# Where the operands of TensorE start in SBUF: every region at 128 above a multiple of 256 bytes, the low halves at 160, 192 or 224

## The reference

```python
for i in range(2):
    h = rms_norm(x, attn_norm[i])
    c_q, c_kv, k_r, q_d, k_d, v_d, g_mla, g_dil = split(h @ w_in[i])
    o_mla = latent_attention(rms_norm(c_q) @ w_uq[i], rms_norm(c_kv) @ w_ukv[i], k_r)
    o_dil = dilated_attention(q_d, k_d, v_d)             # 3 groups x 8 heads of 64
    merged = sigmoid(g_mla) * (o_mla @ w_br_mla[i]) + sigmoid(g_dil) * (o_dil @ w_br_dil[i])
    x = x + merged @ w_out[i]
    h = rms_norm(x, ffn_norm[i])
    if i == 0:
        x = x + (silu(h @ w_gate) * (h @ w_up)) @ w_down              # 1024 -> 3584 -> 1024
    else:
        x = x + sum_e gates[e] * (silu(h @ wg[e]) * (h @ wu[e])) @ wd[e]   # top 2 of 8 experts
    x = x + sigmoid(rms_norm(x, ple_norm[i]) @ ple_w_gate[i]) * (p[i] @ ple_w_proj[i])
return rms_norm(x, final_norm)
```

## The kernel before

| tile | role | before | mod 256 | after | mod 256 |
|---|---|---|---|---|---|
| hi | streams, lines 1918, 1919 | 65664 | 128 | 65664 | 128 |
| lo | streams, line 1944 | 82048 | 128 | 82112 | 192 |
| hT_hi | stationary | 106624 | 128 | 106880 | 128 |
| hT_lo | stationary | 114816 | 128 | 115136 | 192 |
| hs_hi | stationary | 167168 | 0 | 167808 | 128 |
| hs_lo | stationary | 171264 | 0 | 171968 | 192 |
| eaT_hi | stationary | 179456 | 0 | 180352 | 128 |
| eaT_lo | stationary | 181504 | 0 | 182496 | 224 |
| faT_hi | stationary | 158976 | 0 | 159616 | 128 |
| faT_lo | stationary | 163072 | 0 | 163744 | 160 |
| omT_hi | stationary | 204032 | 0 | 204672 | 128 |
| omT_lo | stationary | 129664 | 128 | 130176 | 128 |
| odT, latT, peT (both halves) | stationary | | 0 | | 128 |

## Time and profile before

### The profile page before, as it was taken

The page is one execution under the profiler, slowest core; times in us unless marked ns, Lnnn a source line. Parts: engine busy times, 40 slices in busy tenths (PEclk is TensorE's granted clock), DMA queues, the critical chain, the costliest instruction groups (busy, mean ns, idle before and its releaser), DMA issues.

```text
span 1835.9 us, 27322 instructions
## 1 busy us (share of the span) xinstructions
PE 1827.4 (100%) x8942; PEld 1506.3 (82%) x8942; DVE 1475.3 (80%) x1707; ACT 1245.2 (68%) x1563; POOL 142.0 (8%) x203
## 2 busy tenths in 40 slices
PE   9999999999999999999999999999999999999998
PEld 8888888888888888788888888888888888888887
DVE  6557876566575558779999999999999999999997
ACT  6556664444355556657777787787777777877776
POOL 2400000000002200011101001001010010010000
PEclk9999999999999999999999999999999999999999
DMA  8543345555546543359999999999999999999993
GB/s 331 213 161 115 124 161 192 183 185 193 186 180 238 186 158 118 115 171 375 378 364 362 376 354 398 353 382 374 361 374 374 368 370 361 377 379 359 402 365 125
DMA packets 74065, 511.33 MB, mean 279 GB/s; under 512 B 8280, under 2 KB 8800, under 8 KB 14352
## 3 DMA queue, kind: packets, MB, share of 16 engines
q1 hardware_dynamic: 69072, 493.25, 70.4%
q0 software_dynamic: 4768, 16.95, 3.2%
q10 hardware_dynamic: 160, 0.27, 0.0%
HBM read 501.53 MB, written 8.91 MB: 278 GB/s over the span
## 4 chain that ended last, share of the span: by engine, by line
PE 99%; DVE 1%; issue 0%; ACT 0%; POOL 0%; DVEq 0%; POOLq 0%; ACTq 0%
PE ps L1918 29%; PE ps L1944 29%; PE ps L1919 29%; PE ps L2407 1%; PE ps L2144 1%; PE ps L2120 1%; PE ps L2096 1%; PE ps L2169 1%; PE ps L1957 1%; PE ps L1959 1%; PE ps L1963 1%; PE ps L2106 1%; PE ps L2154 1%; PE ps L1990 1%; PE ps L2547 0%; PE ps L2430 0%
## 5 line engine op out<-in xcount | busy, mean ns | idle before, releaser
L1230 DVE TENSOR_TENSOR lo<-raw,hi 128x1024 fp32r<-128x1024 f32 (+1 forms) x940 | 1103.1, 1211 | 189.1 <-ACT hi L724 185.4
L724 ACT ACTIVATE hi<-raw 128x1024 fp32r<-128x1024 f32 (+1 forms) x940 | 969.0, 1050 | 335.4 <-PE ps L1944 326.3
L1918 PE MATMUL ps<-hi,hs_hi 128*128 128x512 f32 x896 | 360.4, 402 | 0.0
L1919 PE MATMUL ps<-hi,hs_lo 128*128 128x512 f32 x896 | 352.3, 393 | 0.0
L1918 PE MATMUL ps<-hi,hT_hi 128*128 128x512 f32 (+1 forms) x752 | 298.0, 397 | 0.0
L1919 PE MATMUL ps<-hi,hT_lo 128*128 128x512 f32 (+1 forms) x752 | 291.7, 389 | 0.0
L1944 PE MATMUL ps<-lo,hs_hi 128*128 128x512 f32 x896 | 282.0, 395 | 0.0
L1944 PEld LDWEIGHTS ps<-lo,hs_hi 128*128 128x128 f32 x896 | 168.6, 188 | 40.2
L1944 PE MATMUL ps<-lo,hT_hi 128*128 128x512 f32 (+1 forms) x752 | 200.1, 388 | 0.0
L1918 PEld LDWEIGHTS ps<-hi,hs_hi 128*128 128x128 f32 x896 | 168.6, 188 | 38.2
L1919 PEld LDWEIGHTS ps<-hi,hs_lo 128*128 128x128 f32 x896 | 168.9, 189 | 35.4
(11 more groups left out here) (361 smaller groups left out, 1706.5 us busy)
## 6 DMA issues: line engine op xcount, KB each, us to landing
raw<-in_stream SPq DMA_DIRECT2D x466, 1024.0 KB, 6.1
ybuf<-xs POOLq DMA_DIRECT2D x2, 1024.0 KB, 5.5
raw<-in_stream SPq DMA_DIRECT2D x3, 672.0 KB, 8.7
gain<-in_ffn_norm POOLq DMA_DIRECT2D x2, 512.0 KB, 7.9
gain<-in_ple_norm POOLq DMA_DIRECT2D x2, 512.0 KB, 6.8
hbuf<-hnf POOLq DMA_DIRECT2D x1, 1024.0 KB, 9.1
xs<-ybuf POOLq DMA_DIRECT2D x1, 1024.0 KB, 12.5
out_x<-hnat SPq DMA_DIRECT2D x3, 256.0 KB, 2.1
```

The costliest lines, as they stand in the source:

```text
L724: a.activation(dst, src, ACT.Copy).then_inc(hi_done, 1)
L1230: v.tensor_tensor(dst, src, h, ALU.subtract).then_inc(lo_done, 1)
L1918: pe.matmul(o, ah, wh[:, kk, :], start=(first and kk == 0), stop=False)
L1919: pe.matmul(o, al, wh[:, kk, :], start=False, stop=False)
```

## The change

The instructions of all five engines stay the same and in the same order; no tile, loop, wait or transfer is added or taken away. Only start addresses in SBUF move. `region()` now rounds up to 128 above a multiple of 256, which takes the regions qk_odd, Dr, Mr and Tr and all in them from 0 to 128 mod 256. The filler of 64 bytes ahead of `lo` and of `hT_lo` sets these at 192, and one of 192 bytes behind each brings the next tile back to 128. In Dr three low stationary tiles get an offset of their own: `faT_lo` 32, `hs_lo` 64 and `eaT_lo` 96 above the 128 of the others, and the tiles behind them move up by 256 or 512 bytes so that they keep 128.

```diff
@@ -123,7 +123,7 @@
             return t
 
         def region(n):
-            top[0] = (top[0] + 127) // 128 * 128
+            top[0] = (top[0] + 127) // 256 * 256 + 128
             r = top[0]
             top[0] += n
             return r
@@ -131,10 +131,14 @@
 
         raw = sb("raw", [P, RAW, SLAB])
         hi = sb("hi", [P, RING, UNIT], F32R)
+        top[0] += 64
         lo = sb("lo", [P, RING, UNIT], F32R)
+        top[0] += 192
         xs = sb("xs", [P, T, D])
         hT_hi = sb("hT_hi", [P, KD, S], F32R)
+        top[0] += 64
         hT_lo = sb("hT_lo", [P, KD, S], F32R)
+        top[0] += 192
         gain = sb("gain", [P, D])
         glat = sb("glat", [P, LAT])
         om_at = top[0]
@@ -217,28 +221,28 @@
         f_sig = at("f_sig", [P, T, CH], F32, Dr)
         f_act = at("f_act", [P, T, CH], F32, Dr + 4096)
         faT_hi = at("faT_hi", [P, 4, S], F32R, Dr + 8192)
-        faT_lo = at("faT_lo", [P, 4, S], F32R, Dr + 12288)
+        faT_lo = at("faT_lo", [P, 4, S], F32R, Dr + 12288 + 32)
 
         hn_hi = at("hn_hi", [P, T, D], F32R, Dr)
         hn_lo = at("hn_lo", [P, T, D], F32R, Dr + 8192)
         hs_hi = at("hs_hi", [P, KD, P], F32R, Dr + 16384)
-        hs_lo = at("hs_lo", [P, KD, P], F32R, Dr + 20480)
-        e_sig = at("e_sig", [P, CH], F32, Dr + 24576)
-        e_act = at("e_act", [P, CH], F32, Dr + 26624)
-        eaT_hi = at("eaT_hi", [P, 4, P], F32R, Dr + 28672)
-        eaT_lo = at("eaT_lo", [P, 4, P], F32R, Dr + 30720)
+        hs_lo = at("hs_lo", [P, KD, P], F32R, Dr + 20480 + 64)
+        e_sig = at("e_sig", [P, CH], F32, Dr + 24832)
+        e_act = at("e_act", [P, CH], F32, Dr + 26880)
+        eaT_hi = at("eaT_hi", [P, 4, P], F32R, Dr + 28928)
+        eaT_lo = at("eaT_lo", [P, 4, P], F32R, Dr + 30976 + 96)
         eaT2_hi = at("eaT2_hi", [P, 4, P], F32R, Tr + 16384)
         eaT2_lo = at("eaT2_lo", [P, 4, P], F32R, Tr + 18432)
-        y_hi = at("y_hi", [P, D], F32R, Dr + 32768)
-        y_lo = at("y_lo", [P, D], F32R, Dr + 36864)
+        y_hi = at("y_hi", [P, D], F32R, Dr + 33280)
+        y_lo = at("y_lo", [P, D], F32R, Dr + 37376)
         hnf = at("hnf", [P, T, D], F32, Tr + 8192)
         hsn = at("hsn", [P, D], F32, Tr + 16384)
         ysb = at("ysb", [P, D], F32, Tr)
         hbuf = nc.dram_tensor("hbuf", (S + P, D), F32, kind="Internal").ap()
         ybuf = nc.dram_tensor("ybuf", (S + P, D), F32, kind="Internal").ap()
-        sel = at("sel", [P, T, P], F32R, Dr + 40960)
-        selT = at("selT", [P, S], F32R, Dr + 41984)
-        rt0 = Dr + 43008
+        sel = at("sel", [P, T, P], F32R, Dr + 41472)
+        selT = at("selT", [P, S], F32R, Dr + 42496)
+        rt0 = Dr + 43520
         rw = at("rw", [P, KD, NE], F32, rt0)
         rw_hl = at("rw_hl", [P, KD, 2, NE], F32R, rt0 + 256)
         rb = at("rb", [P, NE], F32, rt0 + 768)
@@ -268,9 +272,9 @@
         idx_in = at("idx_in", [P, 1], U32, rt0 + 1696)
         idx_out = at("idx_out", [P, 1], U32, rt0 + 1728)
 
-        pnat = at("pnat", [P, T, PD], F32, Dr + 49152)
-        peT_hi = at("peT_hi", [P, 2, S], F32R, Dr + 51200)
-        peT_lo = at("peT_lo", [P, 2, S], F32R, Dr + 53248)
+        pnat = at("pnat", [P, T, PD], F32, Dr + 49664)
+        peT_hi = at("peT_hi", [P, 2, S], F32R, Dr + 51712)
+        peT_lo = at("peT_lo", [P, 2, S], F32R, Dr + 53760)
         psg = at("psg", [P, T, D], F32, Dr)
         pp = (o_mla, pp1)
 
```

## The result

The changed kernel takes 1844.7 us (median of 7 executions, 1843.98 to 1845.18) against 1837.89: a ratio of 1.0038, with a 95% interval of 1.0026 to 1.0050. It is slower by 6.8 us, where 28 us less were forecast. The profiled execution has a span of 1843.4 us, 7.5 more than before.

A forecast was written before the change was run, and what follows sets the result against it. The prediction took TensorE's matmul sequence as the bound: 24.5 us from hs and eaT, 1.7 from faT and 1.7 from omT and its like sum to 28, so 1837.7 - 28 = 1809.7, or 1810 us; range 1790 to 1842.

The forecast's parts named there:

- What bounds the kernel: Whole kernel: TensorE's sequence of 8,942 matmuls sets the time, PE busy 1827.4 us of a span of 1835.9.
- Addresses as the cause, by their distance mod 256,: 512-column matmuls: moving read and next stationary load interfere by relative address; equal rests give 226.7 ns, others some 231.7.
- What equal rests would give: Experts' hs and eaT 24.5 us, dense FFN's faT 1.7, omT and three like it 1.7: sum 28 us.
- the pricing of the low halves: Lines 1918, 1919 and 1944: offsets of the low tiles cost nothing, 226.7 ns each, so the sum stays 28 us.
- the 336-column projection: First projection of layer 1: blocks at 192 and 128 alternate at 13.3 ns over 140.0, so 64 above is free.
- `omT` with mixed halves at 232.9 ns: Low tile at 128, high at 0: a third loads at equal rests, yet 7 matmuls take 1.63 us.
- `hT` loses its pattern: Slower: any unequal third spoils all stages; experts stay at 232.8 ns, hT loses 13.5 us, giving 1851; chance 0.18.
- One third stays dear: Line 1918 alone costs 232.8 ns, the other two 226.7: a gain of 14, 1824 us; chance 0.17.
- The change doesn't touch the cause: hT is cheap for lying below byte 131,072, faT, hs and eaT stay above: nothing changes, 1838 us; chance 0.12.
- The prediction's help from `omT_lo`: omT_lo, at 128 mod 256 but nearly all above byte 131,072, was not cheap, which favours the half of memory.
- Better than equal rests: Lines 1918 and 1944: a small distance avoids half of what is over 213.3 ns, another 31 us, 1779; chance 0.08.
- The other engines: Experts: DMA would rise from some 370 to 380 GB/s, VectorE from 93% to 95% busy; both hold, little to spare.

The follow-up runs named there:

- all at 128: The kernel before with region() rounding to 128 above a multiple of 256, no fillers, so all 512-column operands start at 128 mod 256: 1812.94 us.
- all at 0: The kernel before with base moved up by 128 bytes and regions rounded to multiples of 256, every operand at 0 mod 256: 1812.08 us.
- second kernel of distances: Against the changed kernel: hi and lo at 128 mod 256, both halves of hT 64 above, hs 32 above, eaT 96 above, faT 64 below; 1848.38 us.

## Why the prediction was wrong

**What bounds the kernel** was right: in every kernel PE is busy throughout, and steps times counts give the time.

**Addresses as the cause, by their distance mod 256,** was right, and is shown by the kernels with all at 128 and all at 0. The rule of the Trainium skill, page "SBUF — State Buffer", section "Who interferes with whom", that TensorE's two read ports are independent and PE never waits on anyone, is not borne out here: with the same instructions in the same order, addresses alone moved the time between 1812 and 1848 us.

**What equal rests would give** was put at 28 us. With truly equal rests it is 24.7 to 25.5 us. The steady 226.7 ns was the right figure, but after small matmuls or a switch to another tile it takes up to a dozen steps to be reached (in the kernel with all at 128, `hs` has means up to 229.7 ns in the first twelve and 226.7 from the thirteenth on), so the means are 227.0 (`eaT`) and 227.7 (`hs`).

**The step that failed is the pricing of the low halves.** For line 1944 I took "64 above costs nothing there" from the 336-column projection, and for line 1918 I extended it to the other direction. With 512 columns a distance of 64 under line 1944 alone gives 232.5 ns with `hs` and 233.6 with `hT`, and takes 23.7 us. The 336-column form was a bad stand-in, because it hardly changes with the addresses: over its 140.0 ns of stream it has between 12.4 and 14.2 ns in all eleven kernels whose steps I took, where the 512-column form has 13.5 to 20.7. A form that doesn't change can show no price. Its two blocks stand 64 apart mod 256 in every one of the kernels, so no run has it with all rests equal, and whether it is insensitive or never at its best stays open. The sum also took the three lines one by one, with 226.7 ns for each. In the changed kernel they measure 233.8, 231.9 and 232.7 ns with `hs` and 231.3, 232.7 and 231.7 with `hT`, behind the lines that were 1918, 1919 and 1944. So even line 1919, whose distance is zero, wasn't at 226.7. The row that was of the right form, `omT` with mixed halves at 232.9 ns, pointed the right way and was given to a rival.

**The rival that came true** is the slower one, `hT` loses its pattern and the experts gain nothing. Its mechanism, that an unequal third spoils the steps of the others, is shown for `lo`, as a settling of about five steps, and in part for the low tiles. Its price of 13.5 us, which gave 1851, was mis-sized: it set the steady 226.7 ns against 232.8, but the mean of `hT` was 228.6 before and 231.9 after, 7.3 us. The steady figure held in the dense FFN alone: in the kernel before `hT` has 227.2 and 227.3 ns from 300 to 500 us, but 230.6 from 0 to 100 us and 231.0 from 500 to 600.

**The other rivals.** "One third stays dear" fell with the kernel in which only the low stationary tiles are off: two thirds are dear there. "The change doesn't touch the cause" fell with all at equal rests, where tiles above byte 131,072 are as cheap as `hT`. The prediction's help from `omT_lo` for it was weaker than it says: by its address 2,688 of its 4,096 bytes lie above that byte, not nearly all, and its high half stood at another rest. "Better than equal rests" found no support at 512 columns.

**The other engines.** VectorE, ScalarE and the DMA didn't become the bound, at 378 GB/s either.

What stays open is how the reads collide. The runs show a cost at 512 columns that depends on the distance mod 256, is least at equality, and carries over for some steps to those whose own distance is zero. They don't show which of the two reads is held, nor for how long.

## What to carry to other kernels

Where TensorE bounds a kernel, streams 512-column float32r blocks without a pause and each has its own weight load, as here, try to let every moving and every stationary operand start at the same rest mod 256, low halves too. It was worth 1.3% here, and one odd moving buffer took 23.7 of the 24.7 us. Price an edit from rows of the same shape as the one it touches: a form that shows no difference may be one that can't. Where several steps alternate, don't price them one by one: look at the steps by their place in the pattern. And take a mean over the stretch for what is lost, not the best steady step.

## What the runs showed of the hardware that was not expected

The 13.3 ns over the stream are not a fixed price of changing the stationary block. With streams of 256 columns and `hT` at equal rests, steps are 120 ns, 13.3 over the 106.7 of the stream. The kernel before, final stage:

```profile
1811.75 0.28 PE L1919 MATMUL ps<-hi,hT_lo 128*128 128x256 f32 x1
...
1812.95 0.28 PE L1919 MATMUL ps<-hi,hT_lo 128*128 128x256 f32 x1
```

Ten steps in 1.20 us. In the second kernel of distances, with `hT` 64 above, the same stage:

```profile
1822.14 0.28 PE L1920 MATMUL ps<-hi,hT_hi 128*128 128x256 f32 x1
...
1823.50 0.28 PE L1920 MATMUL ps<-hi,hT_hi 128*128 128x256 f32 x1
```

Twelve steps in 1.36 us, 113.3 ns each, which is 6.7 over the stream: half of the price. So a distance of 64 above is worse than none with 512 columns and better with 256; whether yet another distance is better still was not tried. There are some hundred matmuls of that width here, which would be 0.6 us and below what a measurement tells.
